# One 128-column matmul per block and level of the gated scan, on a mixed stationary tile

## What is computed

```python
g_f = log_forget(h_ff, lb_f); g_b = log_forget(h_fb, lb_b)
k_f = -jnp.expm1(g_f);        k_b = -jnp.expm1(g_b)
out_f = chunk_scan(q, k_f, g_f, v)
out_b = chunk_scan(q[:, ::-1], k_b[:, ::-1], g_b[:, ::-1], v[:, ::-1])[:, ::-1]
# chunk_scan, written as scores: for t >= s
#   score[t, s] = sum_k q[t, k] * k[s, k] * exp(b[t, k] - b[s, k]),  b = cumsum(g)
#   out[t] = sum_s score[t, s] * v[s]
```

## Time and profile before

| what | us |
|---|---|
| median of 3 runs | 2751.52 |
| lowest, highest | 2750.9, 2759.78 |
| span of the profiled execution | 2759.1 |
| TensorE busy | 2564.6 (93%) |
| VectorE busy | 1033.8 (37%) |
| ScalarE busy | 858.9 (31%) |
| GpSimd busy | 858.6 (31%) |

### The profile page before, as it was taken

The page is one execution under the profiler, slowest core; times in us unless marked ns, Lnnn a source line. Parts: engine busy times, 40 slices in busy tenths (PEclk is TensorE's granted clock), DMA queues, the critical chain, the costliest instruction groups (busy, mean ns, idle before and its releaser), DMA issues.

```text
span 2759.1 us, 32138 instructions
## 1 busy us (share of the span) xinstructions
PE 2564.6 (93%) x12527; PEld 2067.5 (75%) x12527; DVE 1033.8 (37%) x1426; ACT 858.9 (31%) x957; POOL 858.6 (31%) x198
## 2 busy tenths in 40 slices
PE   6999999989999899999998999997989687899996
PEld 4899766768887679986675888875967565688875
DVE  4244333433331033443243333203555643640523
ACT  3212344234332231124432433313145232331320
POOL 2322122324444432212233344442222123244441
PEclk9999999999999999999999999998999889899998
DMA  4322222334443432212233344443322413244441
GB/s 111 77 62 47 47 62 61 77 71 96 91 102 85 96 69 62 62 31 61 62 76 76 76 91 102 89 90 68 77 46 61 77 38 80 51 92 92 100 94 35
DMA packets 202825, 203.04 MB, mean 74 GB/s; under 512 B 14536, under 2 KB 194904, under 8 KB 202712
## 3 DMA queue, kind: packets, MB, share of 16 engines
q1 hardware_dynamic: 202712, 201.45, 34.0%
HBM read 197.21 MB, written 2.11 MB: 72 GB/s over the span
## 4 chain that ended last, share of the span: by engine, by line
PE 77%; DVE 12%; issue 8%; ACT 2%; DVEq 1%; ACTq 0%; DMA 0%; SPq 0%
PE psG L348 22%; PE psG L349 22%; PE psG L350 22%; PE psH L418 2%; PE psH L667 1%; PE psH L687 1%; DVE rms L429 1%; PE psH L607 1%; DVE s_diag L561 1%; DVE ga L1153 1%; DVE h_lo L445 1%; DVE h_tmp L441 1%; DVE Qf L526 1%; DVE Kb L526 1%; DVE Kf L526 1%
## 5 line engine op out<-in xcount | busy, mean ns | idle before, releaser
L2096 POOL TENSOR_TENSOR w_lo<-raw,w_hi 128x2048 fp32r<-128x2048 f32 x186 | 856.9, 4607 | 1849.8 <-ACT w_hi L341 1849.8
L341 ACT CAST w_hi<-raw 128x2048 fp32r<-128x2048 f32 x186 | 354.9, 1909 | 1275.0 <-PE psG L350 1256.8
L348 PE MATMUL psG<-h_hi,w_hi 128*128 128x512 f32 x1640 | 655.4, 400 | 46.3 <-DVE h_lo L445 46.3
L349 PE MATMUL psG<-h_lo,w_hi 128*128 128x512 f32 x1640 | 645.8, 394 | 0.0
L350 PE MATMUL psG<-h_hi,w_lo 128*128 128x512 f32 x1640 | 645.2, 393 | 0.0
L348 PEld LDWEIGHTS psG<-h_hi,w_hi 128*128 128x128 f32 x1640 | 311.6, 190 | 162.5 <-DVE h_lo L445 50.7
L350 PEld LDWEIGHTS psG<-h_hi,w_lo 128*128 128x128 f32 x1640 | 312.1, 190 | 66.5
L349 PEld LDWEIGHTS psG<-h_lo,w_hi 128*128 128x128 f32 x1640 | 312.4, 190 | 61.4 <-issue 0.5
L348 PE MATMUL psG<-hid_hi,w_hi 128*128 128x512 f32 x608 | 244.1, 401 | 0.0
L350 PE MATMUL psG<-hid_hi,w_lo 128*128 128x512 f32 x608 | 240.5, 396 | 0.0
L349 PE MATMUL psG<-hid_lo,w_hi 128*128 128x512 f32 x608 | 240.4, 395 | 0.0
(11 more groups left out here) (388 smaller groups left out, 3096.6 us busy)
## 6 DMA issues: line engine op xcount, KB each, us to landing
raw<-in_w_in_dram SPq DMA_DIRECT2D x122, 512.0 KB, 6.2
raw<-in_w_gate_dram SPq DMA_DIRECT2D x44, 512.0 KB, 5.8
raw<-in_w_up_dram SPq DMA_DIRECT2D x44, 512.0 KB, 5.9
raw<-in_w_down_dram SPq DMA_DIRECT2D x32, 512.0 KB, 5.7
raw<-in_w_ff_in_dram SPq DMA_DIRECT2D x32, 512.0 KB, 6.1
raw<-in_w_ff_out_dram SPq DMA_DIRECT2D x32, 512.0 KB, 6.1
raw<-in_w_o_dram SPq DMA_DIRECT2D x16, 512.0 KB, 5.7
raw<-in_w_down_dram SPq DMA_DIRECT2D x16, 384.0 KB, 4.8
```

What stands on the lines that cost most here:

```text
L341: act.copy(w_hi[:, s, :], raw[:, s, :]).then_inc(hi_done.sem, 1)
L348: pe.matmul(out, a_hi, b_hi, start=first, stop=False)
L349: pe.matmul(out, a_hi, b_lo, start=False, stop=False)
L2096: pool.tensor_tensor(w_lo[:, s, :], raw[:, s, :], w_hi[:, s, :].bitcast(F32), ALU.subtract)\
```

## The change

`Qf` and `Qb` become slots 2 and 0 of one tensor `QQ`, 16 KB apart on each partition. A new tensor `k_mix` holds, for the coming level, Kf in the left half of every group and Kb in the right half; it lies where `s_mate` is written after the last level. For level 0 it is Kf + Kb, made by VectorE. For levels 1 to 7 ScalarE writes it in two copies of 128x1024 (`level_mix`), at the head of its work for units 6 to 12. `mixed_q` describes a moving operand of 128 columns which takes the left half of each group from Qb and the right half from Qf. `level_pe` so has one matmul per head and block. VectorE now waits for a level's matmuls, updates first, the K's ahead of the Q's and the totals last, and copies out of `psH` after that. New semaphores are `lev_k` (both K's are updated) and `mix_cp` (`k_mix` is written), for which TensorE waits from level 1 on.

```diff
--- before.py
+++ after.py
@@ -165,15 +165,16 @@
     iota_t = at("iota_t", 27, [P, P], I32)
     xor = at("xor", 28, [P, P], I32)
 
-    Qf = at("Qf", 0, [P, HEADS, S])
+    QQ = at("QQ", 0, [P, 4, HEADS, S])
+    Qb, Qf = QQ[:, 0], QQ[:, 2]
     Kf = at("Kf", 8, [P, HEADS, S])
-    Qb = at("Qb", 16, [P, HEADS, S])
     Kb = at("Kb", 24, [P, HEADS, S])
     Tx = at("Tx", 32, [P, 2, HEADS * S])
     Ty = at("Ty", 48, [P, 2, HEADS * S // 2])
     s_diag = at("s_diag", 56, [P, HEADS, S])
     b_v = at("b_v", 64, [P, TB, BW])
     s_mate = at("s_mate", 72, [P, HEADS, TB, P])
+    k_mix = at("k_mix", 72, [P, HEADS, S])
     s_far = at("s_far", 32, [P, 2, 2 * TB, P])
     ob = at("ob", 40, [P, HEADS, S])
     a_q = at("a_q", 80, [P, TB, BW])
@@ -292,6 +293,8 @@
     b_tok = sem("b_tok", 2)
     lev_up = sem("lev_up", 10)
     lev_mm = sem("lev_mm", 9)
+    lev_k = sem("lev_k", 6)
+    mix_cp = sem("mix_cp", 7)
     lev_cp = sem("lev_cp", 8)
     mate_cp = sem("mate_cp", 1)
     far_mm = sem("far_mm", HEADS)
@@ -519,12 +522,30 @@
         lg = b.bit_length() - 1
         n = HEADS * S // (2 * b)
         t = totals(lg).rearrange("p d (n two) -> p d n two", two=2)
+        for x, side, d in ((Kf, 0, 0), (Kb, 1, 1), (Qf, 1, 0), (Qb, 0, 1)):
+            part = halves(x, b)[:, :, side, :]
+            mm = dve.tensor_tensor(part, part, t[:, d, :, 1 - side:2 - side].broadcast_to([P, n, b]), ALU.mult)
+            if x is Kb and h < P:
+                mm.then_inc(lev_k.sem, 1)
+        mm.then_inc(lev_up.sem, 1)
         if h < 2 * P:
             dve.tensor_tensor(totals(lg + 1), t[:, :, :, 0], t[:, :, :, 1], ALU.mult)
-        for x, side, d in ((Qf, 1, 0), (Kf, 0, 0), (Qb, 0, 1), (Kb, 1, 1)):
-            part = halves(x, b)[:, :, side, :]
-            mm = dve.tensor_tensor(part, part, t[:, d, :, 1 - side:2 - side].broadcast_to([P, n, b]), ALU.mult)
-        mm.then_inc(lev_up.sem, 1)
+
+    def level_mix(act, layer, lv):
+
+        if lv == 1:
+            act.wait_ge(lev_mm.sem, lev_mm.at(layer, 1))
+        else:
+            act.wait_ge(lev_k.sem, lev_k.at(layer, lv - 1))
+        i = 1 << (lv - 1)
+        act.copy(halves(k_mix, i)[:, :, 0, :], halves(Kf, i)[:, :, 0, :])
+        act.copy(halves(k_mix, i)[:, :, 1, :], halves(Kb, i)[:, :, 1, :]).then_inc(mix_cp.sem, 1)
+
+    def mixed_q(a, blk, i):
+
+        both = QQ[:, 0, a, blk * P:(blk + 1) * P]
+        return bass.AP(both.tensor, both.offset,
+                       [[both.ap[0][0], P], [2 * i, P // (2 * i)], [2 * HEADS * S + i, 2], [1, i]])
 
     def level_pe(pe, layer, lv):
 
@@ -534,23 +555,15 @@
             pe.wait_ge(b_q.sem, b_q.at(layer, 2))
         else:
             pe.wait_ge(lev_cp.sem, lev_cp.at(layer, lv))
+            pe.wait_ge(mix_cp.sem, mix_cp.at(layer, lv))
         for a in range(HEADS):
             for blk in range(TB):
                 c = slice(blk * P, (blk + 1) * P)
-                out = psH[:, a, c]
-                if lv == 0:
-                    pe.matmul(out, Kf[:, a, c], Qf[:, a, c], start=True, stop=False)
-                    mm = pe.matmul(out, Kb[:, a, c], Qf[:, a, c], start=False, stop=True)
-                    continue
-                for k, q, side in ((Kf, Qf, 1), (Kb, Qb, 0)):
-                    cut = "p (n two i) -> p n two i"
-                    i = 1 << (lv - 1)
-                    mm = pe.matmul(out.rearrange(cut, two=2, i=i)[:, :, side, :], k[:, a, c],
-                                   q[:, a, c].rearrange(cut, two=2, i=i)[:, :, side, :], start=True, stop=True)
+                q = Qf[:, a, c] if lv == 0 else mixed_q(a, blk, 1 << (lv - 1))
+                mm = pe.matmul(psH[:, a, c], k_mix[:, a, c], q, start=True, stop=True)
         mm.then_inc(lev_mm.sem, 1)
 
     def level_copy(dve, layer, lv):
-        dve.wait_ge(lev_mm.sem, lev_mm.at(layer, lv + 1))
         if lv:
             dve.memset(small[:, 63:64], 0.0)
         for a in range(HEADS):
@@ -1015,6 +1028,8 @@
                 act.wait_ge(lev_mm.sem, lev_mm.at(l, 9))
                 act.copy(s_mate[:, :, :, :].rearrange("p a s t -> p (a s t)"),
                          psH[:, :, :].rearrange("p a t -> p (a t)")).then_inc(mate_cp.sem, 1)
+            if u < 13:
+                level_mix(act, l, u - 5)
             m, s = um + u // 2, u % 2
             split_hi(act, m + 1, s)
             dst = (b_v, a_q, a_k, a_v)[(u - 6) // 2]
@@ -1100,13 +1115,13 @@
                 t = Tx[:, d, a * S:(a + 1) * S]
                 dve.tensor_scalar(t, t, omlb, lb, ALU.mult, ALU.add)
                 k = (Kf, Kb)[d][:, a, :]
-                mm = dve.tensor_scalar(k, k, omlb, None, ALU.mult)
-        mm.then_inc(lev_up.sem, 1)
-        dve.wait_ge(lev_up.sem, lev_up.at(l, 1))
+                dve.tensor_scalar(k, k, omlb, None, ALU.mult)
+        dve.drain()
+        dve.tensor_tensor(k_mix[:, :, :], Kf[:, :, :], Kb[:, :, :], ALU.add).then_inc(lev_up.sem, 1)
         for lv in range(8):
+            dve.wait_ge(lev_mm.sem, lev_mm.at(l, lv + 1))
+            level_update(dve, 1 << lv)
             level_copy(dve, l, lv)
-            level_update(dve, 1 << lv)
-            dve.wait_ge(lev_up.sem, lev_up.at(l, lv + 2))
         dve.wait_ge(lev_mm.sem, lev_mm.at(l, 9))
         level_update(dve, 2 * P)
         dve.drain()
```

## The result

The changed kernel took 2711.72 us (median of 4 runs, 2706.52 to 2713.03), the kernel before 2752.23 beside it (4 runs, 2750.9 to 2759.78). The ratio is 0.9843 [0.9827, 0.9859]: faster by 40.5 us. The prediction said 2710, with 2699 to 2722 as its range. On another chip, with 15 runs of before and 5 of the changed kernel, the saving was 47.8 us (experiment 5), and by the two profiled executions it was 48.3 (spans 2759.1 and 2710.8).

What follows compares the result with a forecast made beforehand. TensorE, busy 93% of the span, was taken as the bound. Terms sum to -21.5 us a layer, -43.0 in both; the clock gives back 1.8, so 2751.5 - 41.2 = 2710.3 us, range 2699 to 2722.

Steps and rivals of the forecast that it cites:

- The bound: In the gated scan TensorE, busy 93% of the span, has no gap between levels; matmuls it sheds are kernel time.
- Level 0: First level of the scan: 16 fewer matmuls at 0.2235 us, 3.57 us saved a layer, slow clock lasting as before.
- The collision: GpSimd's w_lo holds VectorE's first product after a shortened level; level 7 then gives 0.7 us, not 3.53.
- Rival C: VectorE is not held by w_lo: 2703 us, or 2695 with a free moving operand; chance 0.07.
- Level 1: Moving operand jumps at every column: the level takes 7.48 us, 0.42 more than before.
- upper end: Moving-operand price at single-column jumps: 0.467 us a matmul of two records, from a stationary tile's row; lower end 0.2235.
- Level 2: Moving operand in runs of two columns costs close to contiguous: 3.53 us saved a layer.
- rival B: Every jump of the moving operand pays, 0.96 ns each, level 2 then +2.0 us: 2718 us; chance 0.13.
- D: A jump of the moving operand costs far more than a row shows; at 4 ns, 2770 us; chance 0.03.
- Rival A: The moving operand costs nothing extra; level 1 gives 3.53 less a 1.1 us wait: 2705 us; chance 0.20.
- The covers: VectorE's k_mix sum (2.29 us) and ScalarE's two copies a level (1.0 us each, 2.0 upper end) cost nothing.
- The clock: Ahead of mate the gap grows to 4.8 us, the clock falls in both layers, giving back 1.8 us.

Runs made afterwards that it cites:

- experiment 5: The changed kernel itself, nothing edited, run again on another chip: 2710.54 us against 2758.36 for the kernel before.
- experiment 8: The kernel before with only VectorE's order changed, products ahead of the copies, 32 matmuls a level: 2758.27 us against 2758.36.
- Experiments 1 and 3: 1: changed kernel, masked copies ahead of products, 2705.11 us; 3: changed kernel, GpSimd writing 256 of 2048 w_lo columns for units 8 to 15, 2701.53 us.
- experiment 7: The changed kernel with other stationary and moving column patterns in levels 1 to 7, scores not the reference's: 2740.43 us in one run.
- experiment 4: The changed kernel with the moving operand of levels 1 to 7 read in other fixed patterns, scores not the reference's: 2734.24 us in one run.
- experiment 6: The changed kernel with masked copies ahead of products and level 1's moving operand made contiguous by ScalarE in q_mix: 2700.18 us.

## Why the prediction was right, and where it wasn't

**The bound** was read rightly: TensorE's matmuls went, and the time went with them. Levels 3 to 6 gave 3.57 us each (3.53 predicted), with no wait on `k_mix` anywhere. The contiguous 128-column matmul does cost no more than the 64-column one: 3.49/16 = 0.218 us against 0.2207. Nor was the 64-column price one of interleaving: at level 7 of the kernel before each matmul reads and writes one run of 64 columns, and that level took 7.06 us as the others did. The prediction set the Trainium skill's cycle figures ("TensorE: Matmul & The Clock Gate", Back-to-back issue gap) against its row as if they were for the same thing; the section gives them for the isolated gap, and says that a stream of weight loads and matmuls goes by other spacings. Every matmul here has a weight load of its own.

**Level 0** came out right in the sum of both layers, 2.28 + 5.04 = 7.32 us with 7.1 predicted, but that is luck. The prediction let the slow clock at its start last as long as before. Above the full-clock price of 0.2235 us a matmul, level 0 lost 1.65 and 2.92 us in the two layers before, and 2.94 and 1.45 with the change. Where both are at the full clock the term is exact: 7.17 us for 32 matmuls (layer 0 of experiment 8) and 3.59 or 3.60 for 16 make 3.57 or 3.58.

**The collision** held where the prediction put it, from level 2 on: the stretched first product ending 1.1 us after w_lo (1.2 predicted), mate 13.87 us after level 7's start (14.1), the wait of 4.39 (4.8 in the sum, 4.7 among the signs) put down to s_diag. Experiments 1 and 3 take it away from two sides. Rival C is out. At level 1, where the prediction had VectorE start after w_lo, at t + 7.7, it started at t + 5.5 and was held as well (2.27 us); TensorE didn't wait for it. The Trainium skill ("SBUF — State Buffer", Who interferes with whom) says that a VectorE instruction with two SBUF inputs contends with a GpSimd instruction that reads SBUF, and that one with at most one, outside of the 2-port modes, does not; the traces agree (4.08 and 0.74 us under w_lo).

**Level 1** is the step that failed, by its size: 7.48 us predicted, 5.19 measured, 2.29 a layer and 4.6 in both. I took the upper end "because the row is a read of SBUF by the same engine at the same spacing". The row of 0.2337 us opens a new group of 16 bytes with each column, and its 1.83 ns are what experiment 7 measured for such a stationary tile (7.48 us a level), close to the 1.74 of a moving one. The walk comes back to each group once, and that read is cheaper. The measured value lies between the two ends of the bound; the row that chose between them was near in spacing, but not in how often it opens a group. With 5.19 in it the sum is 41.2 + 4.6 = 45.8 us, against 46.0 in the two scans. Why the second visit to a group costs what it does stays open.

**Level 2** took 3.75 us, not 3.53: 0.26 over levels 3 to 7, rival B in a small way (its term was 2.0). Runs of two give 3.75 or 3.76 us in every profile that has them; from runs of four on nothing is left (3.49). The rest of B is out, and D with it. The Trainium skill ("Advanced Engine Details and Errata", SBUF Cachelines) has two hits on a line as the condition for full speed; the table agrees for every 2nd column (3.55) and runs of two (3.75), and for the walk of level 1, with its two hits apart, it would not have told 5.19 from 7.1.

**Rival A** had the wrong price for level 1, but its wait was real: 16.11 us from level to level in experiment 4, with 16.21 worked out. A free moving operand would have run into the queue of VectorE, which is why experiment 6 reorders VectorE as well.

**The covers** held: VectorE's sum cost nothing, ScalarE's copies took 1.04 to 1.19 us (1.0 taken, 2.0 as the end).

**The clock** gave back 0.53 + 1.38 = 1.9 us at mate, with 1.8 predicted. That it fell in both layers was right too. The closeness of the size is partly luck: 5.3 us was predicted for each, and 5.75 and 4.97 came. Windows of 3 us on the changed kernel, mate of layers 0 and 1 (length, busy time and count of PE, PEld, DVE, ACT and POOL, granted clock, DMA share, GB/s):

```profile
237.00:240.00 3.00, 2.62 (x12) 2.62 (x13) 0.33 (x1) 0.00 (x0) 0.00 (x0) 0.50 0.03 5
1144.00:1147.00 3.00, 3.00 (x18) 3.00 (x18) 0.00 (x0) 0.00 (x0) 0.00 (x0) 0.59 0.03 5
```

**The hit of the time** owes something to chance. The saving was taken off a median of three runs, 2751.5, and the two larger samples of before, on two other chips, gave 2756.5 and 2758.4. The traces save 46.0 us in the scans where I had 41.2, and the low median of before takes up the difference: beside the changed kernel it was 2752.23, and the measured saving 40.5. The prediction also took the profiled execution for the one of 2759.78; in all later runs the time is 1.8 us above the span, so it was one of about 2760.9 that isn't among the three. No term hangs on that.

## What to carry to other kernels

Price a matmul by the rows of its own kind: here fp32 with a new stationary tile each time costs the same for 64 and 128 columns, so two halves in one are a saving of one half, as long as the operand that makes it possible takes at least two columns of each 16-byte group, and takes them one behind the other. The walk of level 1 takes two of each group, but goes to another tensor in between, and pays 1.7 us a level for it. When a stage of the bounding engine gets shorter, lay its neighbours' windows over the new times: what used to come after another engine's long operation now starts under it. Then put first in the queue the work that the other engine does not hold.

## What the runs showed of the hardware

- **TensorE's reads of SBUF.** In the levels measured here a record takes 0.85 ns a column (3.49 us a level) or, for each newly opened group of 16 bytes, about 1.74 ns on the moving and 1.8 ns on the stationary operand, whichever is more; every 8th column costs no more than every 4th (7.26 and 7.13 us a level), and the two operands' costs do not add up (7.45). A second column of a group that was left in between is cheaper than a new group (5.19 us against 7.05). Why it is 1.27 ns a column there stays open.
- **A short gap can drop the clock, and may not.** After the same gap of 3.00 us, level 0 with 16 matmuls took 3.59 to 3.60 us at the full clock in 5 of 16 cases (eight profiles, two layers), and 5.03 to 6.52 in the others. After 1.5 to 1.9 us mate took 3.59 or 3.60 us in 8 of 12 cases, and 5.21 or 5.22 in 4. After 4.1 to 4.4 us it was slow in all 8 (4.97 to 6.01). In level 0 alone two runs can so differ by 2 x 2.9 us, a good part of what runs of one kernel were seen to differ by (4 to 14 us), so a single profiled run doesn't measure a level that follows a gap. What decides between the two after equal gaps stays open.
